# A state-space layer's rounds put in another order: readout first, next matrices two tiles ahead

## The chip, the cores and the metric

The kernel runs on one core of a Trainium2 chip. The metric is device time in microseconds (us) from start to end of one execution; lower is better. Three executions of the kernel before took 2875.77, 2877.4 and 2882.53 us, median 2877.4.

## What is computed

Four layers on 256 tokens of width 2048, all in float32: a convolution with block attention, a sparse attention, differential attention with an MLP, and a state-space (S5) layer with an MLP. Each weight matrix is streamed from memory and split into a high and a low part, so that each product takes three matmuls. The change lies in the S5 layer alone:

```python
def s5_mixer(h, a_re, a_im, log_dt, b_re, b_im, c_re, c_im, d_skip, w_glu):
    ...
    u = h.astype(F32).reshape(B, S, S5_GROUPS, S5_GROUP)      # 128 groups of 16 channels

    def per_sequence(u_s):
        bu_re = jnp.einsum('sgc,gpc->sgp', u_s, bb_re)        # 64 states a group
        bu_im = jnp.einsum('sgc,gpc->sgp', u_s, bb_im)
        _, _, x_re, x_im = lax.associative_scan(
            _scan_combine, (a_seq_re, a_seq_im, bu_re, bu_im), axis=0)
        return jnp.einsum('sgp,gcp->sgc', x_re, cr) - jnp.einsum('sgp,gcp->sgc', x_im, ci)

    y = lax.map(per_sequence, u).reshape(B, S, D)
    y = y + d_skip.astype(F32) * h.astype(F32)
    g = jax.nn.gelu(y).astype(h.dtype)
    val, gate = jnp.split(g @ w_glu, 2, axis=-1)
    return val * jax.nn.sigmoid(gate)
```

## The kernel before

Five instruction streams (`pe`, `act`, `dve`, `pool`, `sp`) are written out by hand and wait for each other on semaphores; nothing reorders them. So the order of the source is the order on each engine, and an instruction that waits holds up all that stand behind it on its engine.

The S5 mixer is worked off in 16 **tiles** of 128 channels, and time is cut into blocks of four steps. The scan runs over 64 blocks on VectorE; what happens within a block of four is a small matrix per group (a "narrow block"). In front of it stands the last down projection of the MLP before, behind it the GLU product `gl0`, whose matmuls take the sixteen finished tiles as their left operand. The loop `for a in range(16)` stands in `pe` (L1054), `act` (L1631), `dve` (L2392) and `pool` (L2583). One pass is called **round** a here; on TensorE (PE) it starts with `drive(a)`.

What is done for one tile, in order, with the names of the buffers as they stand in the trace:

- `drive_matrices(a)` loads the input matrices `WB` (512 KB, two buffers) and `readout_matrices(a)` the output matrices `RD` (640 KB, four buffers) from scratch memory (`s_w`, `s_r`). For tiles 4 to 15 ScalarE (ACT) issues both from its own DMA queue (q10); `RD` of tiles 0 to 3 is loaded ahead of the loop.
- `turn_w(a)`: PE turns `WB` into banks `G2`, `G3`. ACT copies it out (`turned`, into `LAM` or `WT`).
- `within(a)`: PE makes the narrow block from `WB` **and `RD`** (L998), so it waits for both loads (L988, L989). ACT copies it out (`VAR<-T`, 128x128), writes it to memory (`blocks_out`, `s_k`), and SyncE (SP) reads it back in four DMAs as a block-triangular matrix `FD` (`blocks_placed`, L2638; two buffers, so tile a waits for `feed(a-2)`, L2641).
- `drive(a)`: PE, inputs into the states (`T<-US,LAM` or `T<-US,WT`). Then `chain(a)` on VectorE (DVE): rotation, scan, rotation; then GpSimd (POOL) adds the parts (`x_sum`).
- `feed(a)`: PE, `G<-FD,US`. `readout(a)`: PE, `G<-RD,VAR`, waits for `x_sum`.
- `gelu_of(a)`: ACT, from `G` into `VAR`. `turn_y(a)`: PE, turns it. `high_tile(a)` on ACT and `low_tile(a)` on DVE write the operand of `gl0`.
- `decay(a)`: four small ACT copies (`VAR<-KEEP,M`) that the scan of tile a needs.

The waits that the prediction speaks of are these:

```python
988            e.wait_ge(*w_back[a % 2][a])      # within: WB landed
989            e.wait_ge(*r_back[a % 4][a])      # within: RD landed
1016           e.wait_ge(*k_back[a % 2][a])      # feed: FD landed
1037           e.wait_ge(*gelu[a])               # turn_y
2639           e.wait_ge(*k_out[a % 2][a])       # SP, blocks_placed: narrow block written
2641               e.wait_ge(*fd_mm[a - 2])      # SP, blocks_placed: FD buffer read
```

`RD` of tile a+2 is issued by ACT in round a (L1637), right behind `gelu_of(a-2)` in the program, since that tile frees the buffer. SP also loads five of the GLU's weight pieces (`RAW`, 1 MB each) between the `FD` loads.

Of the kernel before, what the change touches and what calls it, by code (L numbers as in the profile page):

```python
# [65 lines left out]
def build_program(nc, t):  # L66
# [281 lines left out]
    def first_half(tag):  # L348
        return half_of[first_chunk[tag], 0]
# [87 lines left out]
    def by_phase(v):  # L437
        return v.rearrange("p (j k) -> p j k", j=4)

    def in_time(v):  # L440
        return v.rearrange("p (k j) -> p j k", j=4)

    def block_bank(a):
        return G[a] if a < 2 else TB[2 + a % 2]
# [7 lines left out]
    def taken(tag, i):  # L452
        if tag == "s5_y":
            return g_low[14 + i]
        if tag == "s5_w":
            return wt_c[15]
        return ev_a[tag, i] if (tag, i) in ev_a.at else ev_d[tag, i]
# [31 lines left out]
    def pe(e):  # L489
# [15 lines left out]
        def mm(out, lhsT, rhs, start, stop):  # L505
            return e.matmul(out, lhsT, rhs, start=start, stop=stop, skip_group_check=True)  # L506
# [467 lines left out]
        def turn_w(a):  # L974
            e.wait_ge(*w_back[a % 2][a])
            if a:
                e.wait_ge(*wt_c[a - 1])
            else:
                for i in range(2):
                    e.wait_ge(*taken(on_pair[1], i))  # L980
            for i in range(2):
                for m in range(4):
                    tk = e.transpose(G[2 + i][:, 128 * m:128 * m + 128], WB[a % 2][:, i, m, :], IDENT)  # L983
            tk.then_inc(*wt_t.up(a))

        def within(a):
            T, W, R = block_bank(a), WB[a % 2], RD[a % 4]
            e.wait_ge(*w_back[a % 2][a])  # L988
            e.wait_ge(*r_back[a % 4][a])  # L989
            if a < 2:  # L990
                e.wait_ge(*taken(on_pair[0], a))
            else:
                e.wait_ge(*(n_h["s", 4 + a] if a < 4 else f_c[a - 2]))
            if a == 0:
                e.wait_ge(*eye["d"])
            for i in range(2):
                for m in range(4):
                    mm(T[32 * m:32 * m + 32, 0:128], W[:, i, m, 96:128], R[:, i, m, 0:128], i == 0, False)  # L998
            for m in range(4):
                tk = mm(T[32 * m:32 * m + 32, 0:32], IDENT[:, 32 * m:32 * m + 32], DD[:, a, :], False, True)  # L1000
            tk.then_inc(*f_mm.up(a))

        def drive(a):
            T = TB[a % 2]
            e.wait_ge(*wt_c[a])
            e.wait_ge(*u_sc[a])
            if a >= 2:
                e.wait_ge(*b_rot[a - 2])
            for i in range(2):
                for m in range(4):  # L1010
                    tk = mm(T[:, 256 * i + 64 * m:256 * i + 64 * m + 64], WT[a % 2][:, i, m, :], US[:, 4 * a + m, :],
                            True, True)
            tk.then_inc(*b_mm.up(a))

        def feed(a):
            e.wait_ge(*k_back[a % 2][a])
            if a >= 2:
                e.wait_ge(*g_low[a - 2])
            for h in range(2):
                for g in range(2):  # L1020
                    m = 2 * g + h
                    tk = mm(G[a % 2][64 * g:64 * g + 64, 128 * h:128 * h + 128], US[:, 4 * a + m, :], FD[a % 2][:, m, :],
                            h == 0, False)
            tk.then_inc(*fd_mm.up(a))

        def readout(a):
            e.wait_ge(*x_sum[a])
            for h in range(2):
                for i in range(2):
                    for g in range(2):  # L1030
                        m = 2 * g + h
                        tk = mm(G[a % 2][64 * g:64 * g + 64, 128 * h:128 * h + 128], ZX[a % 2][:, i, m, :],
                                RD[a % 4][:, i, m, 32:160], False, i == 1)
            tk.then_inc(*y_mm.up(a))

        def turn_y(a):
            e.wait_ge(*gelu[a])
            T, Yg = G[a % 2], YG[a % 2]
            for j in range(4):
                for g in range(2):  # L1040
                    ps = slice(64 * g, 64 * g + 64)
                    tk = mm(T[ps, 256 + 64 * j:320 + 64 * j], Yg[ps, 64 * j:64 * j + 64], IDENT[ps, ps], True, True)
            tk.then_inc(*y_t.up(a))
# [9 lines left out]
        rows("s", TB[1])  # L1053
        for a in range(16):  # L1054
            drive(a)
            if 1 <= a < 15:
                turn_w(a + 1)
                within(a + 1)
            if a >= 2:
                turn_y(a - 2)  # L1060
            if a:
                feed(a - 1)
                readout(a - 1)


        def last_tiles():
# [18 lines left out]
    def act(e):  # L1085
# [16 lines left out]
        def copy(out, in_, scale=1.0):  # L1102
            return e.activation(out, in_, ACT.Copy, scale=scale, bias=0.0)  # L1103
# [4 lines left out]
        def split_next():  # L1108
            n = split[0]
            split[0] += 1  # L1110
            c, h = halves[n]
            N = chunks[c][1][1]
            if h == 0 or c < NR:
                e.wait_ge(*(w_first[c]["c"] if c < NR and h == 0 else w_in[c % NR][c]))
            if n >= RS:
                e.wait_ge(*w_read[n - RS])
            copy(WH[:, n % RS, 0:2 * N], RAW[:, c % NR, h * 2 * N:(h + 1) * 2 * N]).then_inc(*w_hi.up(n))
# [453 lines left out]
        def turned(a):  # L1571
            e.wait_ge(*wt_t[a])
            if a >= 2:
                e.wait_ge(*b_mm[a - 2])
            for i in range(2):
                c = copy(WT[a % 2][:, i, :, :], G[2 + i][:, :].rearrange("p (a b) -> p a b", b=128))
            c.then_inc(*wt_c.up(a))

        def within(a):
            e.wait_ge(*f_mm[a])  # L1580
            if a >= 2:
                e.wait_ge(*k_out[a % 2][a - 2])
            copy(KD[a % 2], block_bank(a)[:, 0:128]).then_inc(*f_c.up(a))

        def blocks_out(a):
            e.wait_ge(*f_c[a])
            e.dma_start(KR[a], KD[a % 2]).then_inc(*k_out[a % 2].up(a, 16))

        def drive_matrices(a):
            e.wait_ge(*sp_w[a])  # L1590
            e.dma_start(WB[a % 2][:, :, :, :], SPW[a]).then_inc(*w_back[a % 2].up(a, 16))

        def readout_matrices(a):
            e.wait_ge(*sp_r[a])
            e.dma_start(RD[a % 4][:, :, :, :], SPR[a]).then_inc(*r_back[a % 4].up(a, 16))

        def decay(a):
            if a >= 2:
                e.wait_ge(*scan[a - 2])
            for m in range(4):  # L1600
                d = copy(MG[a % 2][:, 64 * m:64 * m + 64], KEEP[:, :], M4[:, 4 * a + m:4 * a + m + 1])
            d.then_inc(*mg.up(a))

        def gelu_of(a):
            e.wait_ge(*y_mm[a])
            if a >= 2:
                e.wait_ge(*y_t[a - 2])
            fn(YG[a % 2].rearrange("p (j h c) -> p h j c", j=4, h=2),
               G[a % 2][:, 0:256].rearrange("p (h j c) -> p h j c", h=2, j=4), ACT.Gelu_apprx_tanh).then_inc(*gelu.up(a))

        def high_tile(a):
            e.wait_ge(*y_t[a])
            copy(in_time(A1h[:, a, :]), by_phase(G[a % 2][:, 256:512])).then_inc(*g_hi.up(a))
# [17 lines left out]
        for a in range(16):  # L1631
            if a < 15:
                decay(a + 1)
            if a >= 2:
                gelu_of(a - 2)
                if a < 14:
                    readout_matrices(a + 2)  # L1637
            if 1 <= a < 15:
                turned(a + 1)
                within(a + 1)  # L1640
                blocks_out(a + 1)
                if a < 13:
                    drive_matrices(a + 3)
            if a == 12:
                limit[0] = first_half("gl0") + 2
                for _ in range(2):
                    split_next()
            if a >= 2:
                high_tile(a - 2)


        limit[0] = len(halves)
# [1035 lines left out]
    for program in (pe, act, dve, pool, sp):  # L2688
        program(Count())
# [12 lines left out]
    @block.scalar  # L2702
    def _(eng):
        act(eng)
# [5 lines left out]
    @block.tensor  # L2710
    def _(eng):
        pe(eng)
# [63 lines left out]
```

## Time and profile before

| | |
|---|---|
| median of three executions | 2877.4 us (2875.77 to 2882.53) |
| span of the profiled execution | 2881.1 us |
| PE busy over the span | 99% |
| rounds 2 to 13, `drive(2)` to `drive(14)` | 1897.72 to 1980.69: 83.0 us, 6.9 us a round |
| a round without a wait on PE | 5.52 us (1931.97 to 1937.48) |
| first matmul of `gl0` | 1990.92 |

All times in the trace count from the start of the span. The whole S5 loop is some 100 us of 2881; outside it the change touches nothing. In the loop PE's order is the thing to read: the view of its instructions in order of time gives for each merged piece its start, its length and, in brackets, the idle time before it and who ended that. The granted clock is PE's, 1.00 for 2.4 GHz and 0.50 for 1.2 GHz.

### The profile page before, as it was taken

The numbers are of one execution on the slowest core, as the hardware profiler recorded it, in microseconds if no ns is written. First come the engines' busy times: TensorE is split into PE (matmuls) and PEld (weight loads), VectorE is DVE, ScalarE is ACT, GpSimd is POOL, SyncE is SP. The second block draws the span as 40 slices with busy tenths as digits, with TensorE's granted clock in tenths as the row PEclk, the third lists the DMA queues.
The fourth block names the chain that finished last, engine by engine and source line by source line (L and its number), as shares of the span: only waits on it lengthen the run. The fifth ranks groups of instructions, "written<-read, shape, count | busy, mean of one in ns | idle before, by whom it ended". The sixth has DMA issues, their size and how long they took to land.

```text
span 2881.1 us, 46128 instructions
## 1 busy us (share of the span) xinstructions
PE 2841.2 (99%) x19454; PEld 2585.9 (90%) x19454; DVE 1848.5 (64%) x2543; ACT 1408.0 (49%) x1980; POOL 374.1 (13%) x420
## 2 busy tenths in 40 slices
PE   8999999999999999999999999989999999999998
PEld 8999988998899998999998899878889899988997
DVE  6998655776576665677665666677555555555555
ACT  5434645556555555444444445654545444444444
POOL 0000000000000000007883654122000000000000
PEclk9999999999999999999999999999999999999999
DMA  7555455552555555567776666586655555555553
GB/s 243 191 190 174 137 201 182 190 188 88 175 188 171 171 174 176 191 203 241 237 239 214 237 234 210 200 248 194 199 191 190 194 197 194 190 190 196 197 192 132
DMA packets 288047, 557.99 MB, mean 194 GB/s; under 512 B 25376, under 2 KB 35872, under 8 KB 287584
## 3 DMA queue, kind: packets, MB, share of 16 engines
q1 hardware_dynamic: 275328, 514.49, 54.3%
q0 software_dynamic: 5600, 22.78, 2.0%
q10 hardware_dynamic: 6912, 17.76, 1.8%
q8 instruction: 154, 2.52, 0.4%
q14 instruction: 53, 0.43, 0.0%
HBM read 530.87 MB, written 24.12 MB: 193 GB/s over the span
## 4 chain that ended last, share of the span: by engine, by line
PE 91%; DVE 4%; ACT 2%; DMA 1%; issue 1%; SPq 0%; ACTq 0%; POOL 0%; DVEq 0%
PE G L506 86%; PE T L506 3%; DVE WL L1714 1%; ACT WH L1103 1%; DVE Y L1722 1%; DMA FD<-s_k 1%; PE T L585 1%; DMA s_k<-VAR 1%; DVE XX L1714 0%; PE G L983 0%; ACT L1100 0%; ACT SC_e L1106 0%; DVE ZZ L2374 0%; DVE ST L1795 0%; DVE SC_e L1722 0%
## 5 line engine op out<-in xcount | busy, mean ns | idle before, releaser
L1714 DVE TENSOR_TENSOR WL<-RAW,WH 128x1024 fp32r<-128x1024 f32 (+1 forms) x948 | 1183.1, 1256 | 766.3 <-ACT WH L1103 756.6
L1103 ACT ACTIVATE WH<-RAW 128x1024 fp32r<-128x1024 f32 (+1 forms) x948 | 994.7, 1056 | 1027.7 <-PE G L506 1026.5
L506 PE MATMUL G<-A1h,WH 128*128 128x256 f32 (+1 forms) x2587 | 720.4, 280 | 3.1 <-DVE WL L1714 2.1
L506 PE MATMUL G<-A1l,WH 128*128 128x256 f32 x2560 | 712.9, 278 | 0.0
L506 PE MATMUL G<-A1h,WL 128*128 128x256 f32 x2560 | 711.5, 278 | 0.0
L506 PEld LDWEIGHTS G<-A1h,WH 128*128 128x128 f32 x2587 | 487.3, 189 | 7.0 <-DVE WL L1714 3.1
L506 PEld LDWEIGHTS G<-A1l,WH 128*128 128x128 f32 x2560 | 483.9, 189 | 0.4
L506 PEld LDWEIGHTS G<-A1h,WL 128*128 128x128 f32 x2560 | 482.9, 189 | 0.0
L506 PE MATMUL G<-WH,Bh 128*128 128x512 f32 x1024 | 399.3, 390 | 0.6 <-DVE WL L1714 0.6
L506 PE MATMUL G<-WH,Bl 128*128 128x512 f32 x1024 | 398.5, 389 | 0.0
L506 PE MATMUL G<-WL,Bh 128*128 128x512 f32 x1024 | 398.5, 389 | 0.0
L506 PE MATMUL G<-A3h,WH 128*128 128x256 f32 (+1 forms) x1033 | 283.4, 276 | 0.0
L506 PE MATMUL G<-A3l,WH 128*128 128x256 f32 x1024 | 283.2, 277 | 0.0
L506 PE MATMUL G<-A3h,WL 128*128 128x256 f32 x1024 | 282.7, 276 | 0.0
L506 PEld LDWEIGHTS G<-WH,Bh 128*128 128x128 f32 x1024 | 192.3, 188 | 40.2 <-DVE WL L1714 1.0
L506 PEld LDWEIGHTS G<-WH,Bl 128*128 128x128 f32 x1024 | 192.2, 188 | 40.1
L506 PEld LDWEIGHTS G<-WL,Bh 128*128 128x128 f32 x1024 | 192.3, 188 | 39.0
L506 PE MATMUL G<-WH,A1h 128*128 128x512 f32 (+1 forms) x512 | 203.2, 397 | 0.4 <-DVE WL L1714 0.4
L506 PE MATMUL G<-WH,A1l 128*128 128x512 f32 (+1 forms) x512 | 198.9, 388 | 0.0
L506 PE MATMUL G<-WL,A1h 128*128 128x512 f32 (+1 forms) x512 | 197.6, 386 | 0.0
L506 PEld LDWEIGHTS G<-A3h,WH 128*128 128x128 f32 x1033 | 193.7, 188 | 0.6
L506 PEld LDWEIGHTS G<-A3h,WL 128*128 128x128 f32 x1024 | 192.3, 188 | 0.0
(332 smaller groups left out, 3461.5 us busy)
## 6 DMA issues: line engine op xcount, KB each, us to landing
RAW<-in_mlp_w SPq DMA_DIRECT2D x256, 1024.0 KB, 5.3
RAW<-in_even_w_in SPq DMA_DIRECT2D x52, 1024.0 KB, 5.1
RAW<-in_a_w_in SPq DMA_DIRECT2D x48, 1024.0 KB, 5.2
RAW<-in_b_w_glu SPq DMA_DIRECT2D x32, 1024.0 KB, 5.2
RAW<-in_odd_w_in SPq DMA_DIRECT2D x20, 1024.0 KB, 5.1
RAW<-in_even_w_out SPq DMA_DIRECT2D x16, 1024.0 KB, 5.0
RAW<-in_odd_w_out SPq DMA_DIRECT2D x16, 1024.0 KB, 5.0
RAW<-in_a_w_out SPq DMA_DIRECT2D x16, 1024.0 KB, 5.0
```

The source lines that it names most:

```text
L506: return e.matmul(out, lhsT, rhs, start=start, stop=stop, skip_group_check=True)
L585: m = e.transpose(T[:, 256 * j + 128 * i:256 * j + 128 * i + 128], X[:, i, c:c + 128], IDENT)
L1103: return e.activation(out, in_, ACT.Copy, scale=scale, bias=0.0)
L1714: return e.tensor_tensor(out, a, b, op)
L1722: return e.scalar_tensor_tensor(out=out, in0=a, scalar=s, in1=b, op0=op0, op1=op1)
```

## The change

In `pe`, a round now does `turn_y(a-2)`, `feed(a-1)` and `readout(a-1)` directly behind `drive(a)`, and the turn and the narrow block stand last and are those of tile a+2 rather than a+1. In `act`, `high_tile(a-2)` moves ahead of them, and `turned`, `within`, `blocks_out` and `drive_matrices` are one tile further on. The place of `readout_matrices(a+2)`, behind `gelu_of(a-2)`, is not touched. SP, POOL and DVE are unchanged.

```diff
@@ pe
             drive(a)
-            if 1 <= a < 15:
-                turn_w(a + 1)
-                within(a + 1)
             if a >= 2:
                 turn_y(a - 2)
             if a:
                 feed(a - 1)
                 readout(a - 1)
+            if a < 14:
+                turn_w(a + 2)
+                within(a + 2)
@@ act
                 gelu_of(a - 2)
                 if a < 14:
                     readout_matrices(a + 2)
-            if 1 <= a < 15:
-                turned(a + 1)
-                within(a + 1)
-                blocks_out(a + 1)
-                if a < 13:
-                    drive_matrices(a + 3)
+            if a >= 2:
+                high_tile(a - 2)
+            if a < 14:
+                turned(a + 2)
+                within(a + 2)
+                blocks_out(a + 2)
+                if a < 12:
+                    drive_matrices(a + 4)
             if a == 12:
                 limit[0] = first_half("gl0") + 2
                 for _ in range(2):
                     split_next()
-            if a >= 2:
-                high_tile(a - 2)
```

On TensorE, around round 3. `T1<-US,WT1` is `drive(3)`, `G2`/`G3<-CID,WB0` is `turn_w(4)`, `T2<-RD0,WB0` and `T2<-VAR5` are `within(4)`, `G1<-CID,VAR5` is `turn_y(1)`, the last two are `feed(2)` and `readout(2)`, and `T0<-US,LAM` is `drive(4)`:

```order
-L506 MATMUL T1<-US,WT1 128x64 x8
 L983 MATMUL G2<-CID,WB0 128x128 x4
 L983 MATMUL G3<-CID,WB0 128x128 x4
 L506 MATMUL T2<-RD0,WB0 32x128 x8
 L506 MATMUL T2<-VAR5,CID 32x32 x4
+L506 MATMUL T1<-US,WT1 128x64 x8
 L506 MATMUL G1<-CID,VAR5 64x64 x8
 L506 MATMUL G0<-FD0,US 64x128 x4
 L506 MATMUL G0<-RD2,VAR5 64x128 x8
-L506 MATMUL T0<-US,LAM 128x64 x8
```

The drive has moved from ahead of the turn and the narrow block of tile 4 to behind them; the same two steps are now the last of round 2 and not the second of round 3.

On ScalarE, at the same place. `s5_k<-VAR5` writes the narrow block of tile 4, `WB0<-s5_w` loads the input matrices of tile 6, `VAR5<-G` is a GELU, `A1h<-G1` is `high_tile(1)`, and the last two are `turned(5)`:

```order
 L1587 DMA s5_k<-VAR5 128x128
 L1591 DMA WB0<-s5_w 128x1024
+L1103 ACTIVATE VAR5<-KEEP,M4 128x64 x4
+L1100 ACTIVATE VAR5<-G1 128x2x4x32
+L1595 DMA RD1<-s5_r 128x1280
 L1103 ACTIVATE A1h<-G1 128x4x64
-L1103 ACTIVATE VAR5<-KEEP,M4 128x64 x4
-L1100 ACTIVATE VAR5<-G0 128x2x4x32
-L1595 DMA RD2<-s5_r 128x1280
 L1103 ACTIVATE WT1<-G2 128x512
 L1103 ACTIVATE WT1<-G3 128x512
```

Between the `WB` load of tile 6 and the turned matrices of tile 5, the program before issued `RD` of tile 6; the changed one issues `RD1`, that of tile 5.

## Rows read from the trace of the kernel before

**Rows 1.** TensorE by stretches: us, busy (instructions), granted clock, DMA share, GB/s.

```profile
1886.00:1888.00 2.00, 0.13 (x1) 1.00 1.01 397
1890.00:1892.00 2.00, 2.00 (x12) 0.53 1.05 388
...
1898.00:1912.00 14.00, 13.85 (x208) 1.00 1.02 274
...
1918.00:1920.00 2.00, 2.00 (x12) 0.50 0.94 332
```

**Rows 2.** TensorE in order of time: start, us, instructions [idle before <-releaser].

```profile
1900.99 0.24 PE L506 MATMUL T<-VAR,CID 128*32 128x32 f32 x8
...
1918.01 3.68 PE L506 MATMUL T<-US,WT 128*128 128x64 f32 x16
1921.48 1.91 PE L983 MATMUL G<-CID,WB 128*128 128x128 f32 x8
...
1936.02 0.66 PE L506 MATMUL G<-FD,US 128*64 128x128 f32 x8
1936.51 1.04 PE L506 MATMUL G<-RD,VAR 128*64 128x128 f32 x16
1937.48 2.00 PE L506 MATMUL T<-US,LAM 128*128 128x64 f32 x16
1939.32 1.04 PE L983 MATMUL G<-CID,WB 128*128 128x128 f32 x8
1940.29 0.65 PE L506 MATMUL T<-RD,WB 128*32 128x128 f32 x16
1940.92 0.68 PE L506 MATMUL G<-CID,VAR 64*64 64x64 f32 x16
1944.73 1.12 PE L506 MATMUL G<-FD,US 128*64 128x128 f32 x8 [3.12 <-DMA FD<-s_k]
1945.63 1.92 PE L506 MATMUL G<-RD,VAR 128*64 128x128 f32 x16
...
1967.95 0.64 PE L506 MATMUL T<-RD,WB 128*32 128x128 f32 x16 [0.68 <-issue]
1968.39 0.27 PE L506 MATMUL T<-VAR,CID 128*32 128x32 f32 x8
```

**Rows 3.** ScalarE and its DMA issues in order of time.

```profile
1932.09 0.33 ACTq L1595 DMA_DIRECT2D RD<-s_r  x1
...
1937.46 0.31 ACT L1103 ACTIVATE VAR<-KEEP,M 128x64 f32<-128x64 f32 x1
1937.61 0.38 ACTq L1595 DMA_DIRECT2D RD<-s_r  x1
1938.39 0.36 ACT L1100 ACTIVATE VAR<-G 128x256 f32<-128x256 f32 x1
...
1968.72 0.28 ACT L1103 ACTIVATE VAR<-T 128x128 f32<-128x128 f32 x1 [0.32 <-PE T L506]
1969.03 0.36 ACTq L1587 DMA_DIRECT2D s_k<-VAR  x1
1969.42 0.44 ACTq L1591 DMA_DIRECT2D WB<-s_w  x1
```

**Rows 4.** The RD loads of the loop, and their issue to landing.

```profile
L1595 ACTq DMA_DIRECT2D RD<-s_r x12: 326/326/443, 1898.6 to 1975.1; - x12
DMA to landing us min/median/max: 4.0/6.4/8.9
```

**Rows 5.** Issue to landing of one load each: RD at 1953.42, WB at 1925.20.

```profile
DMA to landing us min/median/max: 6.4/6.4/6.4
DMA to landing us min/median/max: 3.6/3.6/3.6
```

**Rows 6.** DVE and POOL in round 8: first of the chain, last of it, the sum.

```profile
1934.00 0.69 DVE L1714 TENSOR_TENSOR XX<-T,TC 128x512 f32<-128x512 f32 x1 [0.26 <-PE T L506]
1938.80 1.41 POOL L2471 TENSOR_TENSOR VAR<-XX 128x252 f32<-128x252 f32 x2 [3.43 <-DVE XX L1714]
```

## The prediction, made before the changed kernel had run

> **What bounds the kernel now.** PE is busy for 99% of the span, so I first looked for where it is not, in the view of TensorE by stretches, and then read the rounds one by one in the order of time. Three things are to be seen.
>
> First, a round that waits for nothing is PE's own work, with every piece touching the next [rows 2]. From one start to the next it is: drive 1.84 (1937.48 to 1939.32), turn 0.97 (to 1940.29), narrow block 0.63 (to 1940.92), turn_y 0.61, feed 0.49 (1936.02 to 1936.51), readout 0.97 (to 1937.48). The sum is 5.52 us. DVE is nearly as full: before the chain of tile 7 it sits idle for 0.26 us only [rows 6].
>
> Second, rounds 2 to 13 take 83.0 us, which is 12 x 5.52 = 66.2 and 16.8 more. That excess is three waits of `feed` for `FD` (I read 3.19, 3.12 and 2.93 us; the middle one is in [rows 2]) and the half clock that follows such a wait. After the one of 3.19 the clock stood at 0.50 while PE was fully busy [rows 1], and a drive took 3.47 us and a turn 1.91 [rows 2]. So 16.8 us, 0.6% of the kernel, is all that this loop has to give.
>
> Third, the wait that is nearly late already is not `FD` but `RD`. `RD` of tile 9 was issued at 1932.09 [rows 3] and is first read by `within(9)` at 1940.29 [rows 2], a lead of 8.2 us. The twelve loads took 4.0 to 8.9 us, median 6.4 [rows 4]. The one of 8.9 is the 0.68 us of idle at 1967.95 that the profile puts down to "issue" [rows 2].
>
> **The change, part by part.** I count in rounds from `drive(a)` to `drive(a+1)`. No instruction is added or removed, so only waits count.
>
> *The FD wait goes.* The narrow block of tile a leaves ACT at the end of round a-2 and `feed(a)` comes in round a+1, two full rounds and more later; before it was two rounds less the way from `within` to the end of the round. What fills that time is the write, four SP issues and the read. Even the slowest I read (5.8 for the write, 1.3 for the issues, 7.3 for the last read) makes 14.4 us, about two rounds of 7 or 8 us. The other gate, `feed(a-2)` before the buffer is overwritten, leaves two rounds for 1.3 + 7.3 = 8.6 us. Gain: up to 16.8 us.
>
> *turn_y meets its GELU earlier.* Before, turn and narrow block (1.6 us) stood between drive and turn_y. Now only the drive does. ACT begins the round with the copy of the narrow block: PE's narrow block ended at 1968.66, the copy ran from 1968.72 to 1969.00, the two issues behind it until 1969.86 [rows 3]. That is 1.2 us after the end. The decay copies start right then and the GELU 0.93 us after the first of them (1937.46 to 1938.39) and takes 0.36 [rows 3]. So the GELU ends 2.6 us into the round, the drive at 1.84: a wait of 0.75 us. From there PE needs 0.61 + 0.49 + 0.97 + 0.97 to reach the narrow block, at 5.6, and 0.70 for it. The floor of a round in the new order is thus **6.3 us**, not 5.52. The readout's own wait costs nothing: the chain of DVE and the sum of POOL take from 1934.00 to 1940.21 [rows 6], so `x_sum(a-1)` is there 1.84 + 0.2 + 6.2 = 8.2 us after the start of round a-1, which is not later than turn_y and feed of round a where a round is 6.3 or more.
>
> *RD is issued for the round in which it is read.* This decides. `readout_matrices(a+2)` stays behind `gelu_of(a-2)` in round a, but `within(a+2)` has moved from round a+1 into round a. ACT can't reach that issue before it has finished the narrow block of the round before: copy and two issues 1.2 us, and 0.15 to 0.2 from the first decay copy to the `RD` issue (1937.46 to 1937.61) [rows 3], 1.4 us together. So a loop closes: end of `within(a+1)`, 1.4 us to the issue of `RD(a+2)`, landing, `within(a+2)` 0.7 us. A round is **2.1 us plus the landing**. In a round of 5.52 the lead would be 5.52 - 2.1 = 3.4 us, and no load of the twelve was that short [rows 4]. All twelve rounds 2 to 13 pay, since tiles 4 to 15 are loaded so. Behind the waiting PE stand `drive(a+1)`, hence DVE's chain, and ACT's copy of the narrow block, hence the next `RD`.
>
> *How long is the landing?* It is the one cost that the trace does not show in its new place, for `WB` (512 KB) is now issued only 0.6 us ahead of `RD` (640 KB) in the same queue. Bounds: 4.0 is the `RD` load with nothing near it [rows 4]. 8.9 is the worst in rounds of 5.5 us, when the DMA share stands at 1.02 [rows 1]. The nearest row is the load at 1953.42, on a queue that had been quiet, with `WB` 1.1 us ahead: 6.4 [rows 5]. It ran beside an `FD` load and a 1 MB weight piece. In the new order `FD` meets only its tail and a weight piece meets four of the twelve. From the two bare loads, 3.6 for 512 KB [rows 5] and 4.0 for 640 KB, both together need about 4.8 from the `RD` issue if they share the rate of some 390 GB/s [rows 1] (2 us plus 1.15 MB, less the 0.6). I take 5.6, nearer to the load of 6.4 than a bare sum; for the range 4.7 to 6.7.
>
> A rule of the Trainium skill makes it shorter. The page "DMA: Bandwidth & Descriptors", section "Anatomy of one DMA — SWDGE (gpsimd) path", has about 2.0 us fixed plus bytes over 436 GB/s. By it both loads are in 2.0 + 2.7 - 0.6 = 4.1 us after the `RD` issue (an estimate from that page), and the round is at its floor of 6.3. The trace is slower than that fit where it shows a bare load (3.6 against 3.2, 4.0 against 3.5), so I keep it as a rival.
>
> *Clock.* The new round holds two waits, 0.75 and about 1.4 us, of 7.7. A wait of 0.68 left the clock at 1.00; the start of the loop, where PE was nearly idle for 2 us with a short burst before it, brought 0.53 [rows 1]. These lie in between. A round wholly at half clock is 3.5 drive, 0.6 to 1.2 turn_y, 0.9 feed, 1.9 readout, 1.9 turn and 1.1 narrow block, some 10.3 us, longer than the 7.7; the waits absorb 2.2 us of it. Bounds 0 and 12 x 2.6 = 31 us. I take 3, one or two such rounds, since a slow round has no waits and so brings the clock back.
>
> *ACT's two weight splits in round 12* now stand ahead of GELU 11 and `RD(15)`; they are 2 us, part of it inside the wait: 1 us.
>
> **The sum.** Up to the end of `within(3)` PE does the same work as before less `drive(2)`: 1900.99 + 0.24 - 1.84 = 1899.4 is the start of the new round 2. Twelve rounds of 2.1 + 5.6 = 7.7 are 92.4, the splits 1, and the last two rounds as before 10.2 (1980.69 to 1990.92). `gl0` starts at 2003.0 instead of 1990.9, 12 us later; with the clock 15 us. Behind it nothing changes. On the profiled span of 2881.1 that is 2896; on the median of the runs, 3.7 lower, 2892.5.
>
> **The rivals.**
> - *The landing is short and PE at its floor.* With longer rounds the queues are empty, and the loads come in 4.2 us. Twelve rounds of 6.3 are 76 us, `gl0` starts at 1899.4 + 76.1 + 1 + 10.2 = 1986.7, 4 us earlier: 2873. More widely, any landing under 5.3 stays within 0.3% (8.6 us, about what a measurement of this kernel can tell from no change). For it: the bare loads, and the page's fit. Against: `WB` right ahead of each.
> - *The clock stays low.* Each round's waits bring the half clock back, rounds of 9 to 10.3 us: 108 to 124 us against 83, +25 to +43 with the ends as above, 2903 to 2920. For it: the fall after less than 2 us of idle at the loop's start. Against: the 2.2 us of cover.
> - *The FD waits go and nothing takes their place.* This ends on the other side. It needs `RD` to land within 3.4 us of its issue and the GELU within 1.84 us of the round's start; then twelve rounds of 5.52 give 66 us, 15 to 17 us less, 2861. Under a round of 6.0 it would be a measurable gain. Against it stand all twelve landings and the order on ACT.
> - *FD is still late.* If a round stays near 6 us the slowest `FD` way (14.4) could hit once: 1 to 3 us, inside the range.
>
> **How the numbers follow.** Forecast (landings 5.3 to 6.7, clock mostly full, +9 to +25 us): 0.55. Low clock, over +25: 0.15. Short landings, within 0.3%: 0.27. Nothing in its place: 0.03. So slower 0.70, same 0.27, faster 0.03. The predicted time is 2892.5. The range leaves out the floor case and the top of the low clock: landings of 4.7 give 6.8 a round, 0 to +1 us, 2878; at the top three or four slow rounds over landings of 6.7, +33, 2911.
>
> **What would show it.** Right: idle of PE before `T<-RD,WB` of 1 to 2 us in rounds 2 to 13, no idle `<-DMA FD`, a short idle before `G<-CID,VAR 64*64`, and `gl0` starting near 2003. ACT would wait for `PE T` before `VAR<-T` each round. DVE would show idle of about 2 us a round before `XX<-T`. Wrong: `RD` landings near 4 us with rounds of 6.3; or drives of 3.5 us in most rounds. Idle of PE before `G<-FD,US` would say that the lead of `FD` was misread.

## The result, and the profile after

The changed kernel takes 2906.3 us (median of four, 2899.65 to 2908.77) against 2877.3 before (median of four, 2875.77 to 2882.53): 1.0103 times as long, 95% interval 1.0082 to 1.0125. That is 29 us slower, on the side that was forecast and inside the range, and twice the 15 us of the forecast. That is also where the rival of the low clock lay, to which the prediction gave 0.15 (over 25 us, rounds of 9 to 10.3); how much of that rival came true is told below. The profiled executions are 2907.0 and 2881.1 us long, 25.9 apart; `gl0` starts at 2016.76 instead of 1990.92, 25.8 later. So the whole difference lies ahead of `gl0`: rounds 2 to 13 take 107.8 us, 9.0 each, instead of 83.0.

These are TensorE's instructions in order of time in the changed kernel, rounds 4 to 6 (start, us, idle before and who ended it); they answer to [rows 2].

```profile
1915.77 2.00 PE L506 MATMUL T<-US,LAM 128*128 128x64 f32 x16
1918.45 0.68 PE L506 MATMUL G<-CID,VAR 64*64 64x64 f32 x16 [0.68 <-ACT VAR L1100]
1919.06 0.66 PE L506 MATMUL G<-FD,US 128*64 128x128 f32 x8
1919.55 1.04 PE L506 MATMUL G<-RD,VAR 128*64 128x128 f32 x16
1920.52 1.09 PE L983 MATMUL G<-CID,WB 128*128 128x128 f32 x8
1924.95 1.08 PE L506 MATMUL T<-RD,WB 128*32 128x128 f32 x16 [3.33 <-issue]
...
1926.06 3.68 PE L506 MATMUL T<-US,WT 128*128 128x64 f32 x16
1929.67 1.12 PE L506 MATMUL G<-CID,VAR 64*64 64x64 f32 x16
1930.72 1.12 PE L506 MATMUL G<-FD,US 128*64 128x128 f32 x8
1931.63 1.92 PE L506 MATMUL G<-RD,VAR 128*64 128x128 f32 x16
1933.48 1.51 PE L983 MATMUL G<-CID,WB 128*128 128x128 f32 x8
1934.92 0.64 PE L506 MATMUL T<-RD,WB 128*32 128x128 f32 x16
...
1938.56 0.68 PE L506 MATMUL G<-CID,VAR 64*64 64x64 f32 x16 [1.00 <-ACT VAR L1100]
...
1943.55 0.64 PE L506 MATMUL T<-RD,WB 128*32 128x128 f32 x16 [1.82 <-issue]
```

In round 4 TensorE is through with the turn of the next tile at 1921.6 and then stands still for 3.3 us ahead of the narrow block. The profile puts that to "issue", the name that it also gave to the one late `RD` before. The load says who it is: ScalarE issued it at 1917.27 and it took 7.6 us, to 1924.87; the narrow block starts 0.08 us later. In order of time on ScalarE, and under it the time from issue to landing of the `RD` load issued at 1917.27:

```profile
1915.90 0.28 ACT L1103 ACTIVATE VAR<-T 128x128 f32<-128x128 f32 x1 [0.17 <-PE T L506]
1916.21 0.33 ACTq L1587 DMA_DIRECT2D s_k<-VAR  x1
1916.58 0.44 ACTq L1591 DMA_DIRECT2D WB<-s_w  x1
1917.07 0.35 ACT L1103 ACTIVATE VAR<-KEEP,M 128x64 f32<-128x64 f32 x1 [0.89 <-ACT VAR L1103]
1917.27 0.33 ACTq L1595 DMA_DIRECT2D RD<-s_r  x1
1918.04 0.36 ACT L1100 ACTIVATE VAR<-G 128x256 f32<-128x256 f32 x1
```
```profile
DMA to landing us min/median/max: 7.6/7.6/7.6
```

Round 5 shows the second cost. After the wait TensorE runs at half clock: the drive takes 3.6 us and the turn still 1.4, and it reaches the narrow block at 1934.92, 2.6 us after its `RD` had landed (issued 1928.05, 4.3 us). In round 6 the clock is back, so TensorE is early and waits again. The stretches of TensorE (us, busy, granted clock, DMA share, GB/s) say the same and answer to [rows 1]:

```profile
1921.00:1925.00 4.00, 0.67 (x10) 0.89 0.64 237
1926.00:1930.00 4.00, 4.00 (x33) 0.50 0.46 149
1936.00:1944.00 8.00, 5.17 (x79) 1.00 0.79 285
1945.00:1951.00 6.00, 6.00 (x52) 0.50 0.64 219
```

No wait for `FD` is left in rounds 2 to 13. The waits of the loop after its second round, longest totals first (who, line, for whom: us in total, times, longest):

```profile
DVE XX L1714 <- PE T L506: 46.1, 13, 6.7
...
PE T L506 <- issue: 12.4, 7, 3.3
PE G L506 <- ACT VAR L1100: 12.0, 11, 2.4
ACT VAR L1103 <- PE T L506: 10.4, 7, 3.5
```

TensorE waits 12.4 us for `RD` and 12.0 us for the GELU (0.4 of it in round 14); VectorE (DVE) waits 46 us for TensorE, where it was 17 in the loop of before. The `RD` loads of the loop, to compare with [rows 4]:

```profile
L1595 ACTq DMA_DIRECT2D RD<-s_r x12: 326/326/1469, 1900.5 to 1997.0; - x12
DMA to landing us min/median/max: 4.0/5.5/7.6
```

They land sooner than before, 5.5 against 6.4 us. It is the lead that is gone.

### The profile page after: what moved, and what is told of

Its sections match the earlier page's. It is cut to its first block, busy times and chain, and to the rows that moved or that the text cites. A ratio compares the mean times of both kernels' runs of the same rounds, so it can differ in the third digit from the quotient of the medians.

```text
span 2907.0 us, 46128 instructions
## 1 busy us (share of the span) xinstructions
PE 2850.5 (98%) x19454; PEld 2593.2 (89%) x19454; DVE 1847.1 (64%) x2543; ACT 1411.1 (49%) x1980; POOL 376.4 (13%) x420
## 4 chain that ended last, share of the span: by engine, by line
PE 91%; DVE 4%; ACT 3%; issue 2%; ACTq 0%; DMA 0%; DVEq 0%
PE G L506 86%; PE T L506 3%; DVE WL L1714 1%; ACT WH L1103 1%; DVE Y L1722 1%; PE T L585 1%; PE G L983 1%; ACT VAR L1103 0%; ACT L1100 0%; DMA WB<-s_w 0%; ACT SC_e L1106 0%; ACTq L1591 0%; DVE ST L1795 0%; DVE SC_e L1722 0%; DVE XX L1714 0%
```

## The experiments

Each experiment's ratio is taken against runs of the kernel before on the same chip. "Rounds" is the time from `drive(2)` to `drive(14)` in its profiled execution, as read from TensorE's instructions; "waits" are the idle times of TensorE in those rounds. A profile shows one execution, and the last column says how far that one lay from the median of its kernel (before: its span of 2881.1 and the 1.8 us by which a time is longer than a span, against 2877.3). So the rounds of two rows can be compared only to within some 5 to 10 us, and what an edit is worth is read from the ratios; the profiles say which waits there are.

| kernel | ratio to before (95%) | rounds | shortest of them | waits in rounds 2 to 13 | profiled less median |
|---|---|---|---|---|---|
| before | 1 | 83.0 | 5.51 | FD 3.2, 3.1, 2.9; RD 0.7 | +5.6 |
| changed | 1.0103 (1.0082 to 1.0125) | 107.8 | 7.2 | RD 7 times, 12.4; GELU 10 times, 11.6 | +2.4 |
| e1, RD early | 1.0042 (1.0027 to 1.0057) | 87.5 | 6.73 | GELU every round, 1.0 in nine of twelve | -5.4 |
| e2, GELU early | 1.0103 (1.0082 to 1.0125) | 103.3 | 6.1 | RD 8 times, up to 4.2 | -3.0 |
| e3, both | 0.9993 (0.9979 to 1.0006) | 73.7 | 5.66 | RD 0.3, 1.5, 0.9; FD 1.3 | -4.3 |
| e4, filler | 1.0114 (1.0090 to 1.0137) | 112.5 | 7.7 | RD 4 times, up to 2.1; GELU 3 times, up to 3.1 | +7.0 |
| e6, one ahead | 1.0040 (1.0025 to 1.0055) | 89.9 | 6.73 | turned copy 0.54 in every round; GELU 0.39, in three rounds 1.4 to 2.3 | +2.5 |
| e7, before, RD late | 1.0067 (1.0053 to 1.0081) | 95.5 | 5.6 | RD in 11 rounds, 19.3 | -0.5 |
| e8, both, weights late | 0.9976 (0.9966 to 0.9985) | 69.7 | 5.66 | RD 0.3, 1.1 | -2.5 |
| e9, before, weights late | 0.9982 (0.9971 to 0.9993) | 80.4 | 5.51 | FD 3.5, 3.1 | +4.3 |

### e1: the RD load one round earlier

```diff
             if a >= 2:
                 gelu_of(a - 2)
-                if a < 14:
-                    readout_matrices(a + 2)
-            if a >= 2:
                 high_tile(a - 2)
+            if 1 <= a < 13:
+                e.wait_ge(*y_mm[a - 1])
+                readout_matrices(a + 3)
```

> The changed kernel, but the RD load of tile a+3 is issued in round a, behind readout(a-1) and ahead of the turned matrices, so the lead to its narrow block is a round and some 1.7 us more instead of 1.4 us less than a round. Theory A (a round was 2.1 us plus the landing of RD, and the half clock followed those waits): no idle before T<-RD,WB, only the wait of 0.7 us for the GELU is left, rounds 2 to 13 near 6.35 us, 76 us in all against 108 in the changed kernel and 83 before: about 2870 us, ratio to before 0.997. Theory B (the hand-over between TensorE and ScalarE is what lengthens the round, RD is only late with it): rounds stay at 8 to 9 us, 2895 us or more, ratio 1.006 and up.

Measured: 2888.9 us, ratio 1.0042. Every wait before `T<-RD,WB` is gone, the rounds fell from 107.8 to 87.5 us, and the loss against before from 29 us to 11, so `RD`'s lead was the greater part of it. But theory A's 6.35 us a round did not come; nine of the twelve are 6.7 to 6.9, one is 7.2, the other two are 9.8 with the GELU 2.4 us late, once for the table load of the first GELU and once for the two weight splits. One round on TensorE:

```profile
1937.32 2.00 PE L506 MATMUL T<-US,LAM 128*128 128x64 f32 x16
1940.32 0.68 PE L506 MATMUL G<-CID,VAR 64*64 64x64 f32 x16 [1.00 <-ACT VAR L1100]
1940.93 0.66 PE L506 MATMUL G<-FD,US 128*64 128x128 f32 x8
```

The wait for the GELU is 1.0 us. ScalarE still copies the turned matrices (1.08 us) when the narrow block (0.70 us) is done, so its copy of the narrow block, and all behind it up to the GELU, starts 0.3 us later than I had worked it out. The floor of the new order is 6.73 us, not 6.3, and 12 x 6.73 = 81 us is only 2 us under the 83 of before, with all its `FD` waits. The profile is that of the fastest of seven executions, 5.4 us under their median, so it shows less than the 11 us that the median is slower than before. Theory B was wrong on the larger part and right that the hand-over costs something of its own.

### e2: the GELU one round earlier

The call for tile 14 that stood behind the loop falls away, here and in e3.

```diff
-            if a >= 2:
-                gelu_of(a - 2)
-                if a < 14:
-                    readout_matrices(a + 2)
+            if 2 <= a < 14:
+                readout_matrices(a + 2)
             if a >= 2:
                 high_tile(a - 2)
+            if a:
+                gelu_of(a - 1)
```

> The changed kernel, but the GELU of tile a-1 runs in round a, right behind readout(a-1), so turn_y of the next round finds it done; the RD load keeps its place in time, the round in which it is read. Theory A: the wait before turn_y (1.0 us in most rounds) goes, but the round is still 2.1 us plus a landing of 5.5, 7.6 us, and the wait before T<-RD,WB grows by what was saved; the half clock stays too: 95 to 108 us for the twelve rounds, 2889 to 2906 us, ratio 1.004 to 1.010. Theory B: with the hand-over gone the rounds fall to 6 us or less, 2870 us, ratio 0.998 or lower.

Measured: 2906.3 us, ratio 1.0103, the time of the changed kernel itself. The waits for the GELU are gone and those for `RD` grew to 4.2 us; the rounds take 103.3 us. An edit that removes 12 us of waits and gives nothing in the timed runs shows which wait ends last: the one for `RD`.

```profile
1926.55 1.06 PE L506 MATMUL T<-RD,WB 128*32 128x128 f32 x16 [3.86 <-issue]
1927.31 0.41 PE L506 MATMUL T<-VAR,CID 128*32 128x32 f32 x8
1927.65 3.68 PE L506 MATMUL T<-US,WT 128*128 128x64 f32 x16
```

### e3: both

```diff
-            if a >= 2:
-                gelu_of(a - 2)
-                if a < 14:
-                    readout_matrices(a + 2)
             if a >= 2:
                 high_tile(a - 2)
+            if a:
+                gelu_of(a - 1)
+                if a < 13:
+                    readout_matrices(a + 3)
```

> Both edits: GELU and the RD load of tile a+3 right behind readout(a-1). Theory A: nothing is waited for on TensorE, rounds of 5.52 us, twelve in 66 us against 83 before, clock at 1.00 throughout: 2861 us, ratio 0.994. Rival: rounds of 5.5 us press the same bytes through the DMA engines as before, so FD or RD comes late again in two or three rounds, with a half clock behind each: 75 to 83 us, 2870 to 2877 us, ratio 0.997 to 1.000.

Measured: 2876.2 us, ratio 0.9993, no difference from before that can be told. The profiled execution has nine rounds of 5.66 to 6.0 and `gl0` starts at 1979.33, 11.6 us earlier than before, but it was the second fastest of ten, and 2.9 of the 11.6 us lie ahead of round 2. The rival has it: in the quick rounds `RD` and `FD` were late again four times, and the half clock followed two that came within 5 us of each other.

### e4: the waits filled with work

```diff
+        def filler(a, n):
+            e.wait_ge(*f_c[a])
+            for _ in range(n):
+                e.transpose(TB[2 + a % 2][:, 128:256], IDENT, IDENT)
@@ pe, in a round
             drive(a)
+            if 2 <= a < 14:
+                filler(a, 6)
             ...
                 turn_w(a + 2)
+                if a >= 2:
+                    filler(a, 12)
                 within(a + 2)
```

> The changed kernel with idle time filled: TensorE does 6 more transposes of 128x128 between drive and turn_y (0.7 us) and 12 more between the turn and the narrow block (1.5 us) in rounds 2 to 13; their result is read by nobody. If the waits cost more than their length because the half clock follows them: the clock stays at 1.00, rounds are 7.6 to 7.9 us, twelve in 91 to 95 us against 108, 2890 to 2894 us, ratio 1.004 to 1.006, faster with more work. If the clock has little to do with it and the landing alone sets the round: no gain, or up to 5 us more, 2906 to 2912 us, ratio 1.010 to 1.012.

Measured: 2909.0 us, ratio 1.0114; by its interval not to be told from the changed kernel. That is in the span of the second theory (no gain, 1.010 to 1.012), and the clock did not stay at 1.00, as the first needed. Yet the experiment does not settle the price of the clock. Read in slices of 1 us, the time at half clock from round 2 to 13 fell from 34 us to 17, but TensorE's own work had grown to 7.7 us, so a round that still fell to half clock took longer than one of the changed kernel: 10.8 us in rounds 5 and 11, with no wait before its narrow block that could absorb it. The profiled execution was the longest of four, 7 us over their median, so its rounds of 112.5 us overstate the loss too. The end of round 10 and the start of round 11 on TensorE:

```profile
1985.24 0.64 PE L506 MATMUL T<-RD,WB 128*32 128x128 f32 x16 [1.90 <-issue]
1985.67 0.27 PE L506 MATMUL T<-VAR,CID 128*32 128x32 f32 x8
1985.87 3.60 PE L506 MATMUL T<-US,WT 128*128 128x64 f32 x16
1989.26 1.49 PE L1048 MATMUL T<-CID 128*128 128x128 f32 x6
```

### e6: the new order, one tile ahead

```diff
@@ pe (and the same numbers in act)
-            if a < 14:
-                turn_w(a + 2)
-                within(a + 2)
+            if 1 <= a < 15:
+                turn_w(a + 1)
+                within(a + 1)
```

> Half of the change: feed and readout first, turn and narrow block last in the round, but still of the tile one ahead (a+1), on TensorE and ScalarE. RD of tile a+2 is issued in round a and read at the end of round a+1, a lead of more than a round, so it should never be late. If the loss of the changed kernel is the lead of RD, this kernel has no wait before T<-RD,WB; instead FD is short: written at the end of round a and fed in round a+2, one round and 2.5 us later, while write, issues and read took 8 to 14 us before. Each round then waits for FD: rounds of 7.5 to 9 us, 90 to 108 us in all, 2885 to 2905 us, ratio 1.002 to 1.009. If the new order on its own were harmless and only the two tiles ahead cost, rounds would be 6 us, 2870 to 2877 us, ratio 0.998 to 1.000.

Measured: 2887.8 us, ratio 1.0040, rounds 89.9 us. As theory A had it, no wait for `RD`. But my reason for the rest was wrong: `FD` is not late in rounds 2 to 13 either, so that the time fell into the expected span (2885 to 2905 us) was luck. A quick round is 6.73 us because `drive(a+1)` stands right behind the turn and narrow block of its own tile and waits 0.54 us for ScalarE's copy, and turn_y waits 0.39 us for the GELU.

```profile
1938.24 0.68 PE L506 MATMUL G<-CID,VAR 64*64 64x64 f32 x16 [0.39 <-ACT VAR L1100]
...
1942.58 0.66 PE L506 MATMUL T<-US,LAM 128*128 128x64 f32 x4 [0.54 <-ACT LAM L1103]
```

So with the turn last in the round and the GELU in its old place a quick round is 6.73 us both with one tile ahead (e6) and with two (e1), 1.2 more than the 5.52 of before. With the GELU moved as well it is 5.66 (e3, e8).

### e7: the kernel before, with only the RD load late

```diff
                 gelu_of(a - 2)
-                if a < 14:
-                    readout_matrices(a + 2)
             ...
                     drive_matrices(a + 3)
+            if 2 <= a < 14:
+                readout_matrices(a + 2)
```

> The kernel before with one line moved: the RD load of tile a+2 is issued in round a behind ScalarE's copy and write of the narrow block and behind the WB load, some 4.5 us later than before; TensorE's order is that of before. Theory A: this alone closes the same loop (end of a narrow block, 1.3 us to the RD issue, landing 5.5, next narrow block 0.7), so RD is waited for at T<-RD,WB in most rounds: 7.5 us a round and half clock behind the longer waits, 90 to 100 us for the twelve, 2885 to 2898 us, ratio 1.003 to 1.007. Rival (the loss comes from TensorE's new order or the hand-over to ScalarE): within 0.2% of before.

Measured: 2895.5 us, ratio 1.0067, rounds 95.5 us: theory A at the upper end of its span. TensorE's order is untouched and `FD` is never waited for, yet in eleven of twelve rounds it waits for `RD`, and half clock follows six of the seven waits of 1.7 us and more. The loads themselves landed after 5.5 us (median).

```profile
PE T L506 <- issue: 19.3, 11, 3.8
```

This reproduces the loop without the changed order: a late `RD` alone is worth 19 us in the medians, some two thirds of the change's loss.

### e8 and e9: the GLU's weight pieces later

e8 is e3 with this edit, e9 the kernel before with it:

```diff
@@ sp
-                if a in (4, 6, 8, 10):
-                    load(gl0 + (a - 4) // 2)
+                if a in (8, 13, 14, 15):
+                    load(gl0 + (8, 13, 14, 15).index(a))
```

> The kernel with GELU and RD load right behind readout (both edits), and SyncE issues the four weight pieces of the GLU behind the FD loads of tiles 8, 13, 14 and 15 rather than 4, 6, 8 and 10, that is mostly in the last rounds, where RD and WB are loaded no more. If the late RD and FD that were left (1.45, 0.86 and 1.32 us with a half clock behind) come from the weight pieces in the same DMA engines: no wait left, 12 rounds in 67 to 69 us, 4 to 6 us less than with both edits alone, ratio to before 0.994 to 0.997. If they don't: 0.998 to 1.000. Loss possible where the GLU's first product waits for its weights: then up to 5 us more.

> The kernel before with only that edit of the weight pieces (behind FD loads 8, 13, 14, 15). If the three FD waits of before (3.2, 3.1, 2.9 us and the half clock behind) come from the load on the DMA engines, one or two of them go: 5 to 12 us less, ratio 0.996 to 0.998. If the lead of FD is simply too short in the old order, they stay: within 0.1% of before.

Measured: e8 2868.8 us, ratio 0.9976, the fastest kernel here and clear of before; e9 2871.3 us, 0.9982, also clear. The two intervals overlap, so what the new order adds over the weight pieces is not shown by the times. Neither of the two expectations for e8 came: its 0.9976 lies between the span for no wait left (0.994 to 0.997) and the one for no help (0.998 to 1.000). Of e9's three waits one went, as the first expectation had it, at the small end of its 5 to 12 us. The profiles differ: e8 has two waits of 0.3 and 1.1 us, no half clock at all in the loop, and `gl0` starts at 1974.27, 16.7 us earlier than before (13.3 in rounds 2 to 13, 3.4 ahead of them); e9 still has two `FD` waits of 3.5 and 3.1 us with the half clock behind. So in this one profile of the old order the lead of `FD` stays short even with fewer bytes beside it. One round of e8 on TensorE, without a wait:

```profile
1917.63 2.00 PE L506 MATMUL T<-US,LAM 128*128 128x64 f32 x16
1919.56 0.68 PE L506 MATMUL G<-CID,VAR 64*64 64x64 f32 x16
1920.17 0.66 PE L506 MATMUL G<-FD,US 128*64 128x128 f32 x8
1920.66 1.04 PE L506 MATMUL G<-RD,VAR 128*64 128x128 f32 x16
1921.63 1.09 PE L983 MATMUL G<-CID,WB 128*128 128x128 f32 x8
1922.65 0.64 PE L506 MATMUL T<-RD,WB 128*32 128x128 f32 x16
```

## Why the prediction was right, and what it sized wrong

- *What bounds the round.* Right: the end of a narrow block, the `RD` issue, the landing, the next narrow block. e1 takes the cause away and the loss falls from 29 us to 11; e7 puts it into the kernel before and 19 us come (20 and 12 us in the rounds of the profiled executions); e2 shows that the other wait hides behind it.
- *Start of round 2:* 1899.4 forecast, 1898.71 measured. *Last two rounds:* 10.2 forecast, 10.24 measured (2006.52 to 2016.76).
- *Landing:* 5.6 forecast, 5.5 measured (median; the mean of the twelve is 5.55). Part of that is luck: the bare sum of 4.8 does not come out of its terms, since 2 us and 1.15 MB at 390 GB/s less 0.6 are 4.4, and 4.7 with the 2.3 us that the bare loads leave at that rate; the forecast stood on the one load of 6.4. The page "DMA: Bandwidth & Descriptors" of the Trainium skill, section "Anatomy of one DMA — SWDGE (gpsimd) path", gave an estimate of 4.1 by its fit, which it states for loads that GpSimd issues; these are issued by ScalarE. The trace does not agree with it: even the load of round 13, with no `WB` ahead of it, took 4.0 where the fit has 3.5.
- *From the narrow block to the RD issue:* 1.4 forecast, 1.67 in the mean (1.06 to 2.47 over rounds 3 to 13). Two things were missed, the turned copy that ScalarE is still busy with (0.3, as in e1), and `WB` issues that took 0.75 to 1.17 us instead of 0.44 in three rounds. That is 3 us over the loop. The loop as measured is 12 x (1.67 + 5.55 + 0.70) = 95.0 us against 92.4.
- *The clock is the term that was mis-sized.* I took 3 us, "since a slow round has no waits and so brings the clock back". It does bring it back, and just so the next round waits for `RD` again and loses it again. From the rows: in rounds 2, 5, 7 and 11 TensorE reached the narrow block 0.2, 2.6, 1.8 and 2.1 us after `RD` had landed, 6.7 us. In round 13 turn_y started at 2000.06, which at full clock puts the narrow block at 2003.1; it stood at 2005.76, 2.7 us. With a narrow block at half clock this is 9 to 10 us. So the outcome, +29 us, is in the span of the rival "the clock stays low" and over the +9 to +25 of the main forecast, and the rival's mechanism came true in part: five stretches at half clock, 34 of the 107.8 us, where it had every round and the forecast one or two. The time is inside the range because the top of the range allowed three or four such rounds and landings of 6.7. I gave it only 0.15 because the waits were to cover 2.2 us of a slow round; yet rounds 5, 7 and 11 were still 1.8 to 2.6 us late. e4 was to measure the price of the clock directly and did not; it is worked out from these rows and no run shows it by itself.
- *The two weight splits:* 1 us forecast. The wait for GELU 11 was 2.15 us, and it put the narrow block, even at full clock (2003.1), 2 us behind `RD`'s landing at 2001.04. `RD(15)` itself was not held up by the splits as the prediction had it: it was issued at 1997.04, 1.1 us after the narrow block. With these terms (start -0.7, loop +2.6, clock +6.9, splits +1) the forecast comes to within 1 us of the measured start of `gl0`.
- *FD goes.* Right for the changed kernel, but the 16.8 us that rounds 2 to 13 were said to have to give were not reached: e8 wins 13.3 there, since a quick round is 5.66 and not 5.52 and two short waits are left, and its other 3.4 us lie ahead of round 2. There the profile of before was at half clock from 1890 to 1897 and that of e8 from 1886 to 1890; e9, in the order of before, starts round 2 5.4 us earlier too, so this need not come from the order. In time e8 gives only 8 us. The profiled execution of before, 2882.9 as a time, was a long one of its kind (23 executions in the last comparison: 2871.9 to 2885.5, median 2876.7). Its `FD` waits may cost more than those of a usual execution, but that is not shown, for no other execution of it was profiled. The same distance is why the medians differ by 29 us and the profiles by 26.
- *A rival's lower end* was summed too low: rounds of 9 us give +28 us with the ends as stated, not +25.

## What to carry to other kernels

When a step is moved earlier, list all loads that it reads and not only the one that the move is meant to help: here `FD` got more than a round of lead, and `RD`, whose issue stayed in place, lost one and closed a loop through ScalarE. If a load can be issued only after the last step of the round before, and is read in the same round, its whole landing is paid each round; move the issue with its reader, here to directly behind the readout that frees its buffer. And read the waits of more than one execution before you price what can be won.

## What the hardware showed that was not expected

- The half clock did not follow from the length of a wait alone. Each wait of 2.4 us and more in the ten profiles was followed by it. Shorter ones went both ways: it followed 1.40 us at 1916.43 in e6, and 1.32 us at 1923.28 in e3, which came 4.6 us after a wait of 1.45; it did not follow 2.34 us at 1924.76 in e7, while it did the same 2.34 us at 1947.75. A wait of 1.0 us in round after round did not bring it (e1), yet in e6 it came once, at 1971.9, in a run of rounds whose only waits were 0.54 and 0.39 us, of which the round before had the same two:

```profile
1969.51 2.00 PE L506 MATMUL T<-US,LAM 128*128 128x64 f32 x16 [0.54 <-ACT LAM L1103]
1971.90 1.12 PE L506 MATMUL G<-CID,VAR 64*64 64x64 f32 x16 [0.39 <-ACT VAR L1100]
1972.95 1.12 PE L506 MATMUL G<-FD,US 128*64 128x128 f32 x8
1973.86 1.75 PE L506 MATMUL G<-RD,VAR 128*64 128x128 f32 x16
```

- 18 more transposes a round went with half the time at half clock (34 and 17 us, one profile each) and gained nothing.
- Fewer bytes at the same time shortened landings little: `RD` took 6.4 us (median) in rounds of 6.9 us and 5.5 in rounds of 9.0. In the order of e3, with rounds of 5.66, it took 5.6 with the weight pieces in the loop and 5.7 without (e8); in the order of before 6.4 and 5.9 (e9).
